# Expert value panels as the stationary operand in a two-layer PEER decoder trunk

## What is computed

```python
def peer_mixer(h, w_q, subkeys, u_tab, v_tab):
    ...
        q = (xc @ w_q).reshape(C, PEER_HEADS, 2, PEER_HALF)
        s = jnp.einsum("chpd,hpnd->chpn", q, subkeys).astype(jnp.float32)
    ...
        expert = ia * PEER_KEYS + ib
        g = jax.nn.softmax(best_s, axis=-1).astype(xc.dtype)
        act = jax.nn.gelu(jnp.einsum("chkd,cd->chk", u_tab[expert], xc), approximate=False) * g
        return jnp.einsum("chk,chkd->cd", act, v_tab[expert])

        h = modulate(x, ch_norm[i], sh2, sc2)
        x = x + g2[:, None, :] * peer_mixer(h, peer_q_w[i], peer_subkeys[i], peer_u[i], peer_v[i])
```

## Time and profile before

| | |
|---|---|
| median of three runs | 2289.18 us (2288.96 to 2291.25) |
| profiled execution | span 2292.1 us; the page gives no other time for it |
| TensorE busy | 2099.3 us, 92% of the span, 14362 matmuls |
| VectorE, ScalarE, GpSimd busy | 1665.2, 950.4 and 409.0 us |
| HBM | 369.53 MB read, 162 GB/s over the span |

### The profile page before, as it was taken

The page is one execution under the profiler, slowest core; times in us unless marked ns, Lnnn a source line. Parts: engine busy times, 40 slices in busy tenths (PEclk is TensorE's granted clock), DMA queues, the critical chain, the costliest instruction groups (busy, mean ns, idle before and its releaser), DMA issues.

```text
span 2292.1 us, 42769 instructions
## 1 busy us (share of the span) xinstructions
PE 2099.3 (92%) x14362; PEld 1934.8 (84%) x14362; DVE 1665.2 (73%) x2882; ACT 950.4 (41%) x1409; POOL 409.0 (18%) x216
## 2 busy tenths in 40 slices
PE   2877869999999999999969878699999999999998
PEld 2867869999999999998766778699999999999987
DVE  6877995777777777777755579956676666667666
ACT  2224343444444444444433343434444444444443
POOL 1755644000000000000033256430000000000000
PEclk7998989999999999999978989899999999999999
DMA  7763432565565556556622234224444444444453
GB/s 256 257 225 120 154 109 84 174 199 194 193 202 200 193 198 203 193 194 210 210 72 92 74 120 138 101 87 143 156 156 158 163 152 159 161 152 162 157 174 137
DMA packets 102156, 371.39 MB, mean 162 GB/s; under 512 B 11344, under 2 KB 11728, under 8 KB 101584
## 3 DMA queue, kind: packets, MB, share of 16 engines
q1 hardware_dynamic: 94032, 341.26, 44.2%
q0 software_dynamic: 8064, 29.36, 4.0%
HBM read 369.53 MB, written 1.05 MB: 162 GB/s over the span
## 4 chain that ended last, share of the span: by engine, by line
PE 77%; DVE 16%; DVEq 3%; issue 2%; ACT 1%; DMA 1%; SPq 0%; POOL 0%; ACTq 0%; POOLq 0%
PE bank L437 31%; PE bank L390 11%; PE bank L391 11%; PE bank L392 11%; PE bank L449 9%; PE bank L461 3%; DVE arena L966 2%; DVE arena L1119 1%; DVE arena L1036 1%; DVE arena L1049 1%; DVE arena L1038 1%; DMA arena<-in_ada_rows 1%; DVE arena L1033 1%; DVE arena L1046 1%; PE bank L593 1%
## 5 line engine op out<-in xcount | busy, mean ns | idle before, releaser
L390 PE MATMUL bank<-act_hi,w_hi 128*128 128x256 f32 x2732 | 797.9, 292 | 108.2 <-DVE act_lo L1002 53.0
L391 PE MATMUL bank<-act_lo,w_hi 128*128 128x256 f32 x2732 | 787.9, 288 | 0.0
L392 PE MATMUL bank<-act_hi,w_lo 128*128 128x256 f32 x2732 | 786.6, 288 | 0.0
L657 ACT CAST w_hi<-raw 128x1024 fp32r<-128x1024 f32 (+1 forms) x603 | 630.0, 1046 | 326.4 <-PE bank L437 196.5
L942 DVE TENSOR_TENSOR w_lo<-raw,w_hi 128x1024 fp32r<-128x1024 f32 x447 | 547.4, 1225 | 185.0 <-PE bank L437 104.7
L390 PEld LDWEIGHTS bank<-act_hi,w_hi 128*128 128x128 f32 x2732 | 540.0, 198 | 124.3 <-issue 52.4
L391 PEld LDWEIGHTS bank<-act_lo,w_hi 128*128 128x128 f32 x2732 | 540.0, 198 | 7.5
L392 PEld LDWEIGHTS bank<-act_hi,w_lo 128*128 128x128 f32 x2732 | 538.8, 197 | 0.0
L899 POOL TENSOR_TENSOR w_lo<-raw,w_hi 128x1024 fp32r<-128x1024 f32 (+2 forms) x156 | 379.0, 2434 | 437.5 <-PE bank L392 366.8
L437 PE MATMUL bank<-w_hi,wt_hi 128*128 128x512 f32 x1024 | 328.1, 401 | 2.5 <-DVE wt_lo L1181 2.2
L437 PE MATMUL bank<-w_lo,wt_hi 128*128 128x512 f32 x1024 | 318.0, 392 | 0.0
(11 more groups left out here) (167 smaller groups left out, 1535.7 us busy)
## 6 DMA issues: line engine op xcount, KB each, us to landing
raw<-in_u_panels SPq DMA_DIRECT2D x256, 512.0 KB, 3.3
raw<-in_v_panels SPq DMA_DIRECT2D x256, 512.0 KB, 3.2
raw<-in_panels SPq DMA_DIRECT2D x81, 512.0 KB, 3.4
ada<-in_ada_rows POOLq DMA_DIRECT2D x56, 512.0 KB, 4.2
arena<-in_ada_rows SPq DMA_DIRECT2D x40, 512.0 KB, 5.3
raw<-in_panels SPq DMA_DIRECT2D x6, 384.0 KB, 2.9
arena<-in_subkeys SPq DMA_DIRECT2D x2, 1024.0 KB, 5.7
xT<-in_xT SPq DMA_DIRECT2D x1, 1024.0 KB, 6.5
```

The source lines that it names most:

```text
L390: pe.matmul(bank, w_hi[:, slots[0], w], act_hi[:, a], start=(k == 0), stop=False)
L391: pe.matmul(bank, w_hi[:, slots[0], w], act_lo[:, a], start=False, stop=False)
L392: last = pe.matmul(bank, w_lo[:, slots[1], w], act_hi[:, a], start=False, stop=(k == kb - 1))
L657: nc.scalar.copy(w_hi[:, slot, 0:width], raw[:, slot, 0:width]).then_inc(hi_done, 1)
```

## The change

The v panel becomes the stationary operand and the tokens move. `v_panel` now takes the eight blocks of 128 features in turn, each with three matmuls of 128 x 256, so 24 matmuls in place of 12. `YB` then holds features on the partitions: bank k // 2, half k % 2 is block k of `xT`. The copies to `yrow`, the transposes and the 16 additions go; VectorE multiplies the modulation's eight columns by 1/`G_SCALE` (128 x 8) and adds the banks to `xT` in eight operations of 128 x 256. ScalarE starts its squares for both token tiles after the last of them.

```diff
@@ tensor
             def v_panel(stage, j, unroll, it, par, e):
 
                 slots = wait_split(stage, j, unroll, it)
-                for t in range(TT):
-                    a = slice(e * T + t * P, e * T + (t + 1) * P)
-                    for wt, parts in ((wt_hi, (0, 1)), (wt_lo, (0,))):
-                        for v in parts:
-                            for n in range(2):
-                                mm = pe.matmul(YB[2 * t + n][:], wt[:, par, a], (w_hi, w_lo)[v][:, slots[v], n * 512:(n + 1) * 512],
-                                               start=False, stop=False, skip_group_check=True)
+                a = slice(e * T, (e + 1) * T)
+                for k in range(KB):
+                    w = slice(k * P, (k + 1) * P)
+                    y = YB[k // 2][:, k % 2 * T:(k % 2 + 1) * T]
+                    pe.matmul(y, w_hi[:, slots[0], w], wt_hi[:, par, a], start=False, stop=False, skip_group_check=True)
+                    pe.matmul(y, w_hi[:, slots[0], w], wt_lo[:, par, a], start=False, stop=False, skip_group_check=True)
+                    mm = pe.matmul(y, w_lo[:, slots[1], w], wt_hi[:, par, a], start=False, stop=False,
+                                   skip_group_check=True)
                 mm.then_inc(pan_done, 1)
...
-                for t in range(TT):
-                    pe.wait_ge((y0_copied, y1_copied)[t], l + 1)
-                    for g in range(2):
-                        if 2 * t + g >= 2:
-                            pe.wait_ge(yt_added, 4 * l + 2 * t + g - 1)
-                        for k in range(4):
-                            o = t * D + (4 * g + k) * P
-                            mm = pe.transpose(GB[g][:, k * P:(k + 1) * P], yrow[:, o:o + P], ident)
-                        mm.then_inc(yt_done, 1)
@@ scalar
                 last_body(7, True)
-                act.wait_ge(pan_done, ring(f"last{l}", 31)[3] + HI)
-                for n in range(2):
-                    i = nc.scalar.mul(yrow[:, n * 512:(n + 1) * 512], YB[n][:], 1.0 / G_SCALE)
-                i.then_inc(y0_copied, 1)
                 if l == 0:
                     warm(ACT.Sqrt)
+                    act.wait_ge(y_added, 1)
                     for t in range(TT):
-                        act.wait_ge(yt_added, 2 * t + 2)
                         squares(t)
@@ vector
                 wait_product(f"last{l}", 31)
-                for n in range(2, 4):
-                    i = dve.tensor_scalar(yrow[:, n * 512:(n + 1) * 512], YB[n][:], 1.0 / G_SCALE, None, ALU.mult)
-                i.then_inc(y1_copied, 1)
-                for t in range(TT):
-                    for g in range(2):
-                        dve.wait_ge(yt_done, 4 * l + 2 * t + g + 1)
-                        for k in range(4):
...
-                        i.then_inc(yt_added, 1)
+                c = mod_col(l, 5)
+                dve.tensor_scalar(gain[:], mod[:, c:c + KB], 1.0 / G_SCALE, None, ALU.mult)
+                dve.drain()
+                for k in range(KB):
+                    xk = xT[:, k * T:(k + 1) * T]
+                    i = dve.scalar_tensor_tensor(out=xk, in0=YB[k // 2][:, k % 2 * T:(k % 2 + 1) * T],
+                                                 scalar=gain[:, k:k + 1], in1=xk, op0=ALU.mult, op1=ALU.add)
+                i.then_inc(y_added, 1)
                 dve.drain()
                 dve.sem_inc(x_ready, 1)
```

More of the change, by code:

```diff
@@ L188, in program @@
         keys = arena[:, 8192:8192 + PAIRS * KEYS]
-        yrow = arena[:, 0:TT * D]
         ps = [ctx.enter_context(nc.psum_tensor(f"bank{b}", [P, 512], F32)) for b in range(8)]
@@ L249, in program @@
         wt_ready = sem("weighted_gelu_split")
[L250 to L253, removed]
+        y_added = sem("y_added")
         conv_gated = sem("gated_convolution_ready")
```

## The result

The changed kernel takes 2324.73 us (median of four runs, 2323.04 to 2326.16) against 2289.76 us for the kernel before. The ratio is 1.0149, with a 95% interval of 1.0134 to 1.0163: slower, as forecast, and inside the range of 2309 to 2325, by 0.3 us. A second session gave 2326.08 against 2294.14 us, ratio 1.0143 (1.0124 to 1.0162). The profiled span is 2324.5 us, 32.4 more than before.

A forecast was written before the change was run, and what follows sets the result against it. TensorE, busy without a break in mix and nearly so in last, was taken as the bound. 32.0 - 0.8 - 2.5 - 0.4 = +28.3 us on the median of 2289.2 gave 2317.5 us, range 2309 to 2325.

The forecast's parts named there:

- The v panels: Mix and last: 24 matmuls of 128 x 256 replace 12 of 128 x 512, 0.125 us more in each of 256 panels, +32.0 us.
- 0.8 of waits: Last of layer 0: slower panels hide some of TensorE's six small waits for `w_lo`, -0.8 us, bounds 0 and -2.3.
- The rule of the Trainium skill: V panels: matmuls N / 2.4 + 2.5 ns apart, so 2.59 to 2.62 us a panel and +8 us; the prediction followed the rows instead.
- The first rival: V panels: the surplus belongs to what the u panel reads, so v panels nearly keep 2.75 us; +4.8, 2294 us; 6%.
- The second: V panels: the rival that 24 matmuls keep 0.11 us each, so panels take 2.64 us; 2258 us; 3%.
- the fourth: Whole kernel: the rival that TensorE had slack, so only the ends' 3 us show; 2286 us; 2%.
- The end of layer 1: Last v panel to the store: copies, turning and old additions go, so 3.6 us in place of 6.14; -2.5 us.
- The addition: Layer ends: each of eight VectorE additions of 128 x 256 out of a bank takes 0.40 us, 3.3 us in all.
- The end of layer 0: VectorE's release to ScalarE's release: 8.8 us in place of 9.25, sums of squares staying 4.12 us; -0.4, bounds -0.9 and +4.
- The clock falls in TensorE's longer idle time: Layer's end: half of the third rival, idle TensorE loses clock; the rival adds up to 4.4 us, 2322 us; 12%.
- The other half of that rival: Layer's end: the 128 x 8 VectorE operation is caught behind GpSimd; shares the third rival's 2322 us and 12%.

The follow-up runs named there:

- e1_old_roles_24: The kernel before, wt still stationary, with each v matmul of 128 x 512 cut into two of 128 x 256; 2325.43 us, ratio 1.0146.
- e2_half_moving: The changed kernel with 128 tokens moving in each v matmul in place of 256, the other tokens getting no v product; 2530.59 us (one run).
- e3_half_stationary: The changed kernel with 64 columns of each v block stationary in place of 128, half of the features getting no v product; 2289.65 us (one run).

## Why the prediction was right

- **The v panels**, +32.0 forecast less 0.8 of waits, 31.2: measured 32.1. Behind a u panel 2.88 in place of the forecast 2.87, behind a scatter 2.95 as forecast. That the sum is so close is in part luck, as two misses cancel. Mix grew by less than its 12.0 us a layer (96 panels at 0.125), by 11.67 and 11.37. Last of layer 1 grew by 5.08 in place of 4.0: there v panels follow v panels, and the old ones went at 2.73 us (87.36 / 32), not 2.75; the prediction had read only panels behind a u panel or a scatter. The waits in last of layer 0 were indeed absorbed: it grew by 1.1 us less, 3.98. A term that the sum lacked is small: the u panel behind a v panel went from 2.87 to 2.88, some 1 us over 190 panels.
- **The rule of the Trainium skill** (TensorE: Matmul & The Clock Gate, section Back-to-back issue gap: 2.5 ns on top of the columns, for isolated matmuls) would have given 8 us, an estimate. The rows' 0.12 us held, so the measurement decides against it for this type and size. The first rival, that the surplus belongs to the u panel's own operands, is refuted by the new v panels themselves, at 2.88 us, and e1_old_roles_24 shows that it goes with the size of the matmuls. The second, 0.11 us a matmul, is refuted by the timeline, and the fourth, slack on TensorE, by the windows.
- **The end of layer 1**, -2.5 forecast: -2.59. The addition was priced at 0.40 and took 3.23 / 8 = 0.40.
- **The end of layer 0**, -0.4 forecast: +1.72. This is the term that was mis-sized. The step that failed is that the sums of squares keep their 4.12 us; they took 6.31. Its cause stood among the rivals ("The clock falls in TensorE's longer idle time"), with 12% and a price of 2.45 us, but sums at a lowered clock stood in every profile with the new end and no filler, 5.47 to 6.49 us. Some of it should have been in the sum. The other half of that rival, the 128 x 8 operation caught behind GpSimd, did not happen: 0.17 us in both layers.
- **The total**: the span rose by 32.4 against 28.3. Of the 4.1 between them 2.1 are the end of layer 0, 0.9 the v stages, and 1.1 lie in stretches that the change does not touch. The median rose by 35.0 in the first session and by 31.9 in the second; the first difference is the larger since its four runs of the kernel before were short ones for that kernel, 2289.8 against 2292.5 to 2294.1 later.
- **The range** is added up wrongly. The terms at their ends are 28 - 2.3 - 2.8 - 0.9 = 22.0 and 36 - 0 - 1.9 + 4 = 38.1, which on 2289.2 give 2311 to 2327, not 2309 to 2325. The median of 2324.73 fell 0.3 us inside the stated range and that of the second session, 2326.08, just outside, so that the stated range holds the result at all is luck; both lie in the range as its terms give it.

## What to carry to other kernels

Before turning a product round, count matmuls and their moving columns, not only the columns in all: on a TensorE that is busy without a break, twice as many matmuls of half the size made each panel 5% longer here (2.75 to 2.88 us). If a change takes TensorE's work out of a gap that was short, ask what runs behind the gap and at which clock; filler matmuls can buy it back (3.84 us in place of 6.31 here). And read a loss of 1% by stretches between fixed points of the program, since one unchanged stretch alone moved by 4 us between executions.

## What the runs showed of the hardware

- At full clock the v matmuls with 128 stationary columns, in a row, start 0.112 us apart with 128 moving columns, 0.120 with 256 and 0.229 with 512. With 64 stationary columns the 256 go at 0.114; the 512 do not change. Their loads lay never closer than 0.11 us with 128 columns (e2_half_moving), and came down to 0.06 with 64 (e3_half_stationary).
- At half the clock 128 moving columns (last in e2_half_moving) and 256 (the kernel before from 1157.02) both start 0.21 us apart.
- Being busy by the profile did not keep the clock up. With 128 columns moving in the v matmuls the granted clock was 0.50 in last for 149 us at 149.00 us busy; with 256 it was 1.00 in the same stage. This is one execution of one kernel.
- Matmuls of zeros (128 x 256) held the clock here: behind 36 of them the sums of squares took 3.84 us at a granted clock of 1.00, behind an idle stretch of 4.66 us 6.31 at 0.59.
- Shorter idle pieces did not lower the clock every time: behind the transposes of the old end, with the same idle pieces, the same sums took 4.12 us at 1.00 or 5.46 at 0.69.
